# Starting the input projection on half of the blocks, and sharing the preparation of x between ScalarE and VectorE

## The reference, cut to what matters

```
mod = silu(c) @ w_ada + b_ada                       # 6 parts of 1024 columns
sh1, s1, g1, sh2, s2, g2 = split(mod, 6)
h = (x * rsqrt(mean(x*x) + EPS) * norm1_g) * (1 + s1) + sh1
z = h @ w_in                                        # 1024 -> 6144 columns
a_val, a_gate, u_b, s_x, s_b, s_c, z_ga, z_gb, z_gc = split(z, ...)
```

## Time and profile before

| | us |
|---|---|
| median of 3 runs | 895.85 |
| lowest and highest | 894.61, 896.27 |
| the profiled execution's own time | 894.56 |
| its span, first to last instruction | 892.5 |
| mean granted TensorE clock | 0.97 |

### The profile page before, as it was taken

How to read it: one execution, slowest core, us unless ns; L and a number is a source line. 1 busy time by engine, 2 the same in 40 slices (tenths; PEclk the granted TensorE clock), 3 DMA queues, 4 the chain that set the end, 5 groups by cost and what they waited for, 6 DMA issues and landing times.

```text
span 892.5 us, 15049 instructions
## 1 busy us (share of the span) xinstructions
PE 826.4 (93%) x5111; PEld 709.7 (80%) x5111; DVE 691.7 (78%) x942; ACT 473.0 (53%) x556; POOL 51.2 (6%) x58
## 2 busy tenths in 40 slices
PE   7799999999999999999999989999999999999800
PEld 2499999999889999899677968888888888888700
DVE  0772657799777997599358798999999989998648
ACT  4642444233443221632223358888888888888532
POOL 0002000000000000230000010001000100010040
PEclk9999999999999999999999899999999999999955
DMA  9868535544554431124831289968988999999352
GB/s 331 274 196 315 171 95 162 169 129 157 163 166 142 150 118 48 55 88 121 261 129 72 94 322 373 401 259 308 384 308 301 330 399 400 396 398 400 150 214 95
DMA packets 91106, 201.82 MB, mean 226 GB/s; under 512 B 8775, under 2 KB 13383, under 8 KB 91028
## 3 DMA queue, kind: packets, MB, share of 16 engines
q1 hardware_dynamic: 78795, 165.29, 52.5%
q0 software_dynamic: 4960, 17.89, 5.6%
q10 hardware_dynamic: 7307, 18.03, 5.5%
HBM read 183.00 MB, written 18.91 MB: 226 GB/s over the span
## 4 chain that ended last, share of the span: by engine, by line
PE 82%; DVE 10%; DMA 2%; issue 2%; ACT 2%; SPq 1%; ACTq 0%; POOL 0%; DVEq 0%; POOLq 0%
PE ps L748 31%; PE ps L599 13%; PE ps L601 13%; PE ps L600 13%; PE ps L828 3%; DVE w_lo L1448 2%; PE ps L934 2%; DMA region_a<-in_x_prompt_dram 2%; PE ps L780 2%; PE ps L627 1%; PE ps L628 1%; ACT w_hi L1035 1%; PE ps L890 1%; PE ps L963 1%; DVE region_b L1985 1%
## 5 line engine op out<-in xcount | busy, mean ns | idle before, releaser
L1448 DVE TENSOR_TENSOR w_lo<-raw,w_hi 128x1024 fp32r<-128x1024 f32 x210 | 251.1, 1223 | 99.6 <-ACT w_hi L1035 96.4
L1035 ACT ACTIVATE w_hi<-raw 128x1024 fp32r<-128x1024 f32 x210 | 215.8, 1056 | 201.8 <-PE ps L748 151.8
L599 PE MATMUL ps<-w_hi,hT_hi 128*128 128x512 f32 (+1 forms) x512 | 206.0, 402 | 5.1 <-DVE hT_lo L1448 3.6
L601 PE MATMUL ps<-w_hi,hT_lo 128*128 128x512 f32 (+1 forms) x512 | 202.7, 396 | 0.0
L600 PE MATMUL ps<-w_lo,hT_hi 128*128 128x512 f32 (+1 forms) x512 | 202.0, 395 | 0.0
L748 PE MATMUL ps<-hT_hi,w_hi 128*128 128x260 f32 x768 | 156.5, 285 | 2.7 <-DVE w_lo L1448 2.4
L748 PE MATMUL ps<-hT_lo,w_hi 128*128 128x260 f32 x768 | 155.0, 283 | 0.0
L748 PE MATMUL ps<-hT_hi,w_lo 128*128 128x260 f32 x768 | 154.8, 283 | 0.0
L748 PEld LDWEIGHTS ps<-hT_hi,w_hi 128*128 128x128 f32 x768 | 118.7, 189 | 6.6 <-DVE w_lo L1448 6.2
L748 PEld LDWEIGHTS ps<-hT_lo,w_hi 128*128 128x128 f32 x768 | 119.4, 190 | 0.0
L748 PEld LDWEIGHTS ps<-hT_hi,w_lo 128*128 128x128 f32 x768 | 118.8, 189 | 0.0
(11 more groups left out here) (297 smaller groups left out, 787.8 us busy)
## 6 DMA issues: line engine op xcount, KB each, us to landing
raw<-in_exp_w_dram SPq DMA_DIRECT2D x96, 512.0 KB
region_a<-in_exp_w_dram SPq DMA_DIRECT2D x80, 512.0 KB
raw<-in_w_in_dram SPq DMA_DIRECT2D x48, 512.0 KB
raw<-in_w_ada_dram SPq DMA_DIRECT2D x38, 512.0 KB
expert_rows<-region_b ACTq DMA_DIRECT2D x18, 512.0 KB, 6.4
region_b<-in_exp_w_dram SPq DMA_DIRECT2D x16, 512.0 KB
region_b<-in_w_ada_dram SPq DMA_DIRECT2D x9, 512.0 KB, 10.3
expert_rows<-region_a POOLq DMA_DIRECT2D x8, 512.0 KB, 8.8
```

What stands on the lines that cost most here:

```text
L599: pe.matmul(out, pairs[0], moving[0], start=start, stop=False)
L601: return pe.matmul(out, pairs[1], moving[0], start=False, stop=stop)
L1035: act.activation(w_hi[:, split_slot(n), :], place, ACT.Copy).then_inc(hi_done, 1)
L1448: return dve.tensor_tensor(out, whole, first.bitcast(F32), ALU.subtract)
```

## The change

Three things are done. (1) The quarters 4 to 11 are numbered anew: 4 is the first quarter of z0, 5 to 8 are a3, 9 to 11 the other quarters of z0. PE runs z0's quarter 0 for three column tiles, then a3 (in bank 6, which belongs to the fourth tile), then quarter 1 for two tiles, the turning of a3, and then the rest. Since quarter 4 keeps its ring slot until the fourth tile has used it, the parts of quarter 8 go to the still empty blocks 6 and 7 of `hT_hi` and `hT_lo`. (2) The squares of row tiles 1 and 3 go to DVE, the scalings of row tiles 3 and 4 go to ACT, the copies of the turned blocks 4-7 (`turned_x_late`) to DVE. (3) The three queues are written anew around this. The diff, cut to what takes part:

```diff
+ACT_SQUARES = (4, 0, 2)
+DVE_SQUARES = (1, 3)
+def item(n):
+    if 4 <= n < 12:
+        return ("z", 0, 0) if n == 4 else ("a", 3, n - 5) if n < 9 else ("z", 0, n - 8)
+    return ITEMS[n // 4] + (n % 4,)
...
+        def split_place(n):
+            if n == 8:
+                return hT_hi[:, 6:8, 0:COLS], hT_lo[:, 6:8, 0:COLS]
+            return w_hi[:, split_slot(n), :], w_lo[:, split_slot(n), :]
...
@@ TensorE
             ada_quarter(0, 4)
-            ada_quarter(1, 4)
             for k in range(4, KD):
                 pe.wait_ge(xT_out, k - 3)
                 turn_x(k, k - 4)
+            ada_quarter(1, 4)
             ada_quarter(2, 4)
             ada_quarter(3, 4)
-            pe.wait_ge(xT_out, KD)
+            pe.wait_ge(xT_out, 4)
+            pe.wait_ge(xT_late, 4)
             turn_params()
-            ada_quarter(4, 7)
-            ada_quarter(5, 7)
             pe.wait_ge(fold_ready, 1)
             for g in range(3):
-                t = turn_mod(g, 0, 36 * g)
+                t = turn_mod(g, 6, 36 * g)
             t.then_inc(modT_done, 1)
-            ada_quarter(6, 7)
-            ada_quarter(7, 7)
...
+            z_quarter(0, 0, (0, 1, 2))
+            for n in range(5, 9):
+                ada_quarter(n, 6)
+            z_quarter(0, 1, (0, 1))
+            turn_mod(3, 7, 0).then_inc(modT_done, 1)
+            z_quarter(0, 1, (2,))
+            z_quarter(0, 0, (3,))
+            z_quarter(0, 1, (3,))
+            z_quarter(0, 2)
+            z_quarter(0, 3)
@@ ScalarE
-            for n, i in enumerate((4, 0, 1, 2, 3)):
+            for i, junk in zip(ACT_SQUARES, (square_junk, conf_raw.rearrange("p a b -> p (a b)"), later_junk)):
                 act.wait_ge(x_landed[i], 16)
...
+            act.wait_ge(rstd_ready, 1)
+            for t in (3, 4):
+                act.activation(x_in[0:rows(t), t, :], x_in[0:rows(t), t, :], ACT.Copy, scale=sums[0:rows(t), 3, t:t + 1]).then_inc(xn_ready, 1)
...
-            hi(0)
-            hi(1)
             for k in range(4):
                 turned_x(k)
             native_out(1)
-            hi(2)
-            hi(3)
-            for k in range(4, KD):
-                turned_x(k)
-            hi(4)
-            hi(5)
+            for n in range(6):
+                hi(n)
+            act.wait_ge(xT_out, 4)
+            input_sampled(0)
+            input_prompt(0)
+            input_prompt(1)
             hi(6)
             hi(7)
-            act.wait_ge(xT_out, KD)
-            input_sampled(0)
-            input_prompt(0)
-            hi(8)
-            input_prompt(1)
+            act.wait_ge(xT_late, 4)
             input_prompt(2)
             input_prompt(3)
+            hi(8)
             hi(9)
             input_sampled(1)
             for k in range(4, KD):
                 input_prompt(k)
-            hi(10)
-            hi(11)
-            for n in range(N_HEAD + 4, N_HEAD + 7):
+            for n in range(10, N_HEAD + 7):
                 hi(n)
@@ VectorE
+            def turned_x_late(k):
+                dve.wait_ge(xT_done, k + 1)
+                dve.tensor_copy(xnT[:, k, :], ps[:, k % 4, :]).then_inc(xT_late, 1)
+            for i, junk in zip(DVE_SQUARES, (xnT[:, 0:2, :], xnT[:, 2:4, :])):
+                dve.wait_ge(x_landed[i], 16)
+                dve.scalar_tensor_tensor(junk.rearrange("p a b -> p (a b)"), x_in[:, i, :], 1.0, x_in[:, i, :], ALU.mult, ALU.mult,
+                                         accum_out=sums[:, 0, i:i + 1]).then_inc(ssq_ready, 1)
             mean_squares()
             norm_root()
-            for t in range(NTILE):
+            for t in range(3):
                 dve.tensor_scalar(x_in[0:rows(t), t, :], x_in[0:rows(t), t, :], sums[0:rows(t), 3, t:t + 1], None, ALU.mult).then_inc(xn_ready, 1)
-            for n in range(5):
+            lo(0)
+            for k in range(4, KD):
+                turned_x_late(k)
+            for n in range(1, 4):
                 lo(n)
             params_out()
             mod_group(2)
-            lo(5)
-            lo(6)
-            lo(7)
+            lo(4)
             scale_out(0)
             sampled_input(0)
             prompt_sum(0)
             sampled_rest(0)
             prompt_rest(0)
-            lo(8)
             prompt_sum(1)
             prompt_rest(1)
+            for n in range(5, 8):
+                lo(n)
+            prompt_sum(2)
+            prompt_rest(2)
+            lo(8)
+            lo(9)
+            prompt_sum(3)
+            prompt_rest(3)
             mod_group(3)
-            for k in range(2, 4):
-                prompt_sum(k)
-                prompt_rest(k)
-            lo(9)
             scale_out(1)
             sampled_input(1)
             prompt_sum(4)
             sampled_rest(1)
             prompt_rest(4)
-            for k in range(5, KD):
+            prompt_sum(5)
+            prompt_rest(5)
+            lo(10)
+            for k in range(6, KD):
                 prompt_sum(k)
                 prompt_rest(k)
-            lo(10)
             lo(11)
```

More of the change, by code:

```diff
@@ L603, in split_weights @@
             def split_weights(n, k):
-                return slot(w_hi, split_slot(n), k), slot(w_lo, split_slot(n), k)
+                if n == 8:
+                    return split_place(n)
+                return tuple(place.rearrange("p (k n) -> p k n", k=k) for place in split_place(n))
             for m in range(4):
@@ L707, in _, with z_quarter @@
                 turn_x(k, k - 4)
+            ada_quarter(1, 4)
             ada_quarter(2, 4)
             ada_quarter(3, 4)
[L710 removed]
+            pe.wait_ge(xT_out, 4)
+            pe.wait_ge(xT_late, 4)
             turn_params()
[L712 to L713 removed]
             pe.wait_ge(fold_ready, 1)
             for g in range(3):
[L716 removed]
+                t = turn_mod(g, 6, 36 * g)
             t.then_inc(modT_done, 1)
[L718 to L723 removed]
+            def z_quarter(g, q, units=range(4)):
+                n = z_number(g, q)
                 pe.wait_ge(lo_done, n + 1)
                 hi, lo = split_weights(n, 2)
[L726 removed]
+                for m in units:
                     ms = slice(m * P, (m + 1) * P)
@@ L730, in z_quarter @@
                         pe.wait_ge(set_free[m], g + 1)
-                        if m == 2 and g == 0:
-                            turn_mod(3, 6, 0).then_inc(modT_done, 1)
-                        elif m == 2 and ITEMS[n // 4 - 1][0] == "a":
+                        if g == 0 and m == 0:
+                            pe.wait_ge(scaleT_ready, 1)
+                        elif m == 2 and g and ITEMS[n // 4 - 1][0] == "a":
                             pe.wait_ge(mod_ready, ITEMS[n // 4 - 1][1] - G_NAT + 1)
@@ L750, in z_quarter @@
                         mm.then_inc(z_done, 1)
-                mm.then_inc(quarter_used, 1)
-            for i in range(G_HEAD - G_NAT, len(ITEMS)):
+                if 3 in units:
+                    mm.then_inc(quarter_used, 1)
+            z_quarter(0, 0, (0, 1, 2))
[8 more added lines that the diff above has]
+            z_quarter(0, 3)
+            for i in range(G_HEAD - G_NAT + 1, len(ITEMS)):
                 kind, g = ITEMS[i]
@@ L1032, in hi @@
                 act.wait_ge(ready, count)
-                if splits(n) > SPLIT or turn is not None:
-                    act.wait_ge(quarter_used, splits(n) - SPLIT if turn is None else turn * TURN + (splits(n) - SPLIT))
-                act.activation(w_hi[:, split_slot(n), :], place, ACT.Copy).then_inc(hi_done, 1)
+                if turn is not None:
+                    act.wait_ge(quarter_used, turn * TURN + (splits(n) - SPLIT))
+                elif splits(n) > SPLIT and n != 8:
+                    act.wait_ge(quarter_used, splits(n) - SPLIT)
+                if n == 8:
+                    place = place.rearrange("p (k n) -> p k n", k=2)
+                act.activation(split_place(n)[0], place, ACT.Copy).then_inc(hi_done, 1)
             act.wait_ge(ld_c, 32)
@@ L1454, in lo @@
                 dve.wait_ge(hi_done, count)
-                rest(w_lo[:, split_slot(n), :], raw_place(n)[0], w_hi[:, split_slot(n), :]).then_inc(lo_done, 1)
+                hi_part, lo_part = split_place(n)
+                whole = raw_place(n)[0]
+                if n == 8:
+                    whole = whole.rearrange("p (k n) -> p k n", k=2)
+                rest(lo_part, whole, hi_part).then_inc(lo_done, 1)
             dve.memset(cT[:, :, 16:C_LO].bitcast(F32), 0.0)
@@ L1527, in prompt_sum @@
             def prompt_sum(k):
-                dve.wait_ge(xT_out, k + 1)
+                if k < 4:
+                    dve.wait_ge(xT_out, k + 1)
+                else:
+                    dve.wait_ge(xT_late, k - 3)
                 if k >= 2:
```

37 lines of the change are left out of this document (20 added, 17 removed).

## The result

The changed kernel takes 906.98 us (median of 4 runs, 906.71 to 908.24) against 896.0 for the kernel before beside it (4 runs): ratio 1.0143, 95% interval 1.0124 to 1.0162 (the ratios here are the record's estimates from the fast runs; the quotient of the two medians is 1.0123). That is 11.1 us more than the 895.85 from which the prediction started (11.0 more than the kernel beside it), where 7.6 was forecast, and 0.4 above the range. The profiled execution took 906.95 with a span of 904.9, so the span grew by 12.4.

The account below looks back on a forecast made before the run. PE was taken as the bound (93% busy, 82% of the chain), so z0's end moves the kernel's: 7.0 us later, plus 0.6 for a possible second clock fall, 7.6. From 895.85 that gives 903.4, range 899.5 to 906.6.

Parts of the forecast that it names:

- Part 2: First high part: hi(0) stands behind four ACT copies and native_out(1), so turn_x(4) starts at 32.09 instead of 30.40.
- 1.1 won has become 1.7 lost: At turn_x(4): the 1.1 us won by turning x earlier becomes 1.7 lost through the wait for lo(0).
- Part 4: Blocks 0-3 ahead of the scale's second half, up to z0's end: quarter 2 starts at 67.1, z0 ends at 78.6.
- I take it at half, 0.6: Possible extra clock fall after the new standstill at 27.7 to 31.2, which would raise 7.0 to 8.2; counted at half.
- (b): Clock fall to 1.2 GHz after the standstill of 42.4 to 45.7 ahead of z0, costing 1.7 us as before.
- my walk: Row durations put in the new queue order up to z0's end: 7.0 us later, thought good to about 0.1 us.
- rival B: Clock stays at 1.2 GHz over the sparse stretch of 30 to 44: 9.9 us later, 905.8; chance 0.18.
- later waits are on engines that shift along with it: After z0: whatever moves the end of z0 moves the end of the kernel by as much.
- From `lo(12)` on all are again well ahead of PE: Late quarters of z0: loads and low parts there come ahead of PE's need, so loads are costed at nothing.
- C: Rival: lo(0) costs no wait, so z0 ends 0.6 to 2.1 us faster, 893.7 to 895.2; chance 0.07.
- D: Rival: the loss is taken back later, at mixers or routing; time within 1.8 us of before; chance 0.05.
- The rule on transposes: Skill's rule that transposes don't count for the full clock; the forecast saw clock 1.00 over 1.7 us of transposes against it.

Follow-up runs that it names:

- e2: Changed kernel with hi(0) and hi(1) put back ahead of ACT's four copies of turned blocks: 904.39 us, ratio 1.013 to the kernel before.
- e3_pe_busy: Changed kernel with spare PE transposes (28, 16 and 26) in its three long standstills: 903.91 us, ratio 1.0122 to the kernel before.
- e10: Changed kernel with spare transposes in three standstills and the seven small DMA issues behind ACT's copies of z0: 902.29 us, ratio 1.0073.
- e3_again: Changed kernel with spare transposes in three standstills, run once more unchanged: 905.13 us, ratio 1.0105 to the kernel before.
- e5: Changed kernel with hi(0), hi(1) ahead of ACT's copies, seven issues behind z0's copies, spare transposes (16 and 26): 898.09 us, ratio 1.0033.
- e8: Changed kernel with hi(0), hi(1), lo(1) and hi(10) earlier, seven issues behind z0's copies, spare transposes (13 and 26): 895.93 us, ratio 1.0007.
- after: The changed kernel itself, against the kernel before: 906.98 us, ratio 1.0143.
- e6_again: Kernel before with 18 spare transposes ahead of z0, run once more for a second profile: 890.17 us (1 run).
- e6_before_busy: Kernel before with 18 spare transposes in its standstill ahead of z0: 893.85 us, ratio 0.9991.
- e1: Changed kernel with ACT's seven small DMA issues moved behind its copies of z0: 905.13 us, ratio 1.0129 to the kernel before.
- e4: Changed kernel with the two router bias loads issued ahead of the two router weight loads: 905.17 us (1 run).
- c1: The changed kernel once more, unchanged, for a second profile: 907.14 us, ratio 1.0132 to the kernel before.
- e9: Kernel before with shared squares and scalings, and hi(8) and lo(8) one place earlier each: 892.99 us, ratio 0.9977.

## Why the prediction was wrong in its size

**Right: sign, mechanism and the single steps.** Predicted and measured starts: row sums 21.94 / 21.88 (DVE's square with its accumulator ended as estimated from its nearest row); turning of x 25.67 / 25.61; `hi(0)` 28.85 / 28.71; `lo(0)` 29.9 / 29.78; ada 0 31.16 / 31.15; `turn_x(4)` 32.09 / 32.21. Part 2, "1.1 won has become 1.7 lost", is borne out by e2, where two lines take the wait away and z2 comes 2.8 earlier at the same loss by the clock. In Part 4 `lo(9)` and `lo(10)` wait for ACT's `hi`, and PE stands 1.80 before quarter 2, forecast 1.9. Behind z1's start the old trace follows, shifted.

**Wrong in size: the clock.** The term "I take it at half, 0.6" and the single fall of (b). After the new standstill of 3.57 us a fall did come, and a second came at 38.7 in ada 1 to 3. The steps drift from there on: late copies 32.8 / 33.30, ada 1 36.5 (35.3 and one `lo`) / 37.55, `mod_group(2)` 41.1 / 43.56, `scale_out(0)` 42.9 / 45.39, z0 45.7 / 48.46, quarter 2 67.1 / 70.01. z0 ended 10.1 late, 2.5 more than the 7.6 of the forecast. Not all of it is the clock. The forecast had counted one and a half falls at 7.6 - 5.4 = 2.2. By e3_pe_busy, which had none, they cost 3.6 at the end of z0; by my walk, fed with the three observed falls (9.6) and with none (5.4), 4.2. So this term was 1.4 to 2.0 too small. The rest, 0.5 to 1.1, is the walk's own: e3_pe_busy ended z0 6.6 late, where the walk without a fall has 5.4. That the walk met the old order to 0.1 did not carry over to the new one. It was rival B's effect in part: low in two pieces of the sparse stretch, but not throughout.

**Priced as before: the small issues, in "later waits are on engines that shift along with it".** The 2.9 us ahead of z1 come from ACT, whose seven issues stand between its last high part and the copies of z0. ACT did shift along: its first issue came at 76.17 in place of 66.23, 9.9 late where z0's end was 10.1 late. What did not stay the same was one issue's length, 3.94 for 0.60. At the old length the copies would have begun 3.3 earlier, at 80.6, and the first bank would have been free at 81.4, ahead of z0's end at 81.80. I walked the queues to z0's end, counting compute alone on ACT, and so did not see that only 0.25 us lay between these issues and a standstill in the kernel before; the sentence "From `lo(12)` on all are again well ahead of PE" passes over it too. The 3.94 could not be read from the trace of before. e10 against e3_again prices the standstill at 2.8 in the medians.

**The sum.** Predicted 7.6, and 2.5 by which z0 ended later than forecast (1.4 to 2.0 of it the clock), and 2.9 for z1's standstill, less 0.6 that comes back later: 12.4, the growth of the span. The medians grew by 11.1; the profiled execution of before ran 1.3 under the 895.85 of the prediction, and the clock's losses differ that much between executions.

**The rivals.** C (no wait at `lo(0)`, 0.6 to 2.1 us faster) can be judged by e5 and e8, in which `lo(0)` is done early and the rest is mended as well: 1.0033 and 1.0007, no faster than before. By my walk e8's z0 would end 0.4 us earlier than that of the kernel before; in the trace z2 starts 1.6 later, 1.0 of it by the spare transposes. D (taken back later) is out: only 0.7 came back.

**The rule on transposes.** The Trainium skill, "TensorE: Matmul & The Clock Gate", section "Part 4: PE-mode transpose", says that they don't count as activity for the full clock. The runs do not settle it. Against it: the clock rose while PE did transposes alone, in after at about 35.3 at the end of sixteen, in e3_again, e10 and e8 at 42.4 to 47.0 near the end of the 26, and it was 1.00 over the whole stretch in e3_pe_busy, e5 and e6_again. For it: in e3_again, e10 and e8 the clock fell 0.3 to 0.5 us after the 26 had begun, behind other short transposes, though PE was not idle.

Not tried: the order of groups alone in the old queues of ACT and DVE.

## What to carry to other kernels

In a stage where engines hand work to one another, price a change of order by who stands ahead of whom in each queue: two `hi` behind four copies cost 2.8 us at z2, while squares and scalings moved from one engine to the other changed the time by 0.2%. Walk on until every queue, DMA issues included, is back where it was relative to the others, not only to the point where the bound engine has enough work; and note how much slack each wait there has (0.25 us ahead of z1 here), since a slack that small won't cover an issue that takes longer. Count each new standstill of PE of about 2 us or more as its length and a probable fall of the clock, some 1.7 us or more each here, and don't believe a difference of 0.3% from four runs a side. Filler work on PE can overrun: 26 spare transposes took 3.06 us at the full clock and 4.72 with a fall in them, and then held up what they were to bridge by 1.0 us.

## What the hardware did unexpectedly

- **One small DMA issue held ACT's queue for anything from 0.37 to 8.70 us.** First in line 0.37; behind the router weights, ahead of z0's copies, 0.60 to 1.35 in the old order and 2.05 to 3.94 in the new one; behind z0's copies 7.58 to 8.70 in either order. Ahead of the copies its length went with how closely SP's four loads came before it (3 us ahead: 0.60 to 1.35; 1.5: 2.05 and 2.26; none: 3.33 to 3.94). The cause is not shown.
- **The falls of PE's clock are not fixed by the kernel.** The same queues lost 5.4 and 6.8 us (after), 5.0 and 0.0 (e6_before_busy), 0.0 and 1.7 (e3_pe_busy) within 24 to 120 us. After a standstill of 1.8 us before quarter 2 the clock fell in e1, e2, e4, c1 and e10 and not in after, e3_pe_busy, e3_again and e5; before z0 of the kernel before it fell after 2.43. In e6_before_busy and e9 it fell at 38 to 39, after a standstill of 1.1, where five other executions of the old order, with the same standstill, kept 1.00. Behind 120 us, where no queue was changed, single executions lost 0 to 6.6 us. That the spread of one kernel's times, some 3 us either way, comes from this fits but was not shown: from 24 us on, the two profiled executions of e6_before_busy's kernel lost 11.6 and 1.6 us to the clock and took 898.18 and 890.17, but those of after lost 10.3 and 11.9 and took the same.
